# Relative bias rows of both sample attentions: loaded in the prompt attention from the Pool queue and kept on chip

## The reference, cut to what matters

```
bias = jnp.moveaxis(bias_tab[rel_bucket(jnp.maximum(dist, 0))], -1, -2)
logit = jnp.einsum('nqhe,nqkhe->nqhk', q, kg) + bias
p = jax.nn.softmax(logit, axis=-1)
return jnp.einsum('nqhk,nqkhe->nqhe', p, vg)
```

## Time and profile before

| what | value |
|---|---|
| median of the runs | 3127.01 us (3124.59 to 3127.49) |
| the profiled execution | 3129.59 us, of which the span is 3127.8 us |
| PE busy | 2659.0 us (85% of the span) |
| DVE / ACT / POOL busy | 1136.5 / 666.8 / 366.8 us |
| PE's share of the chain that ended last | 40% (the MLP, at the end) |
| prompt attention | 1251 to 1449 us, PE busy 166.18 us of 198 |
| sample attention B | 1449 to 1589 us, PE busy 79.74 us of 140 |
| sample attention C | 1589 to 1834 us, PE busy 160.65 us of 245 |

### The profile page before, as it was taken

The page is one execution under the profiler, slowest core; times in us unless marked ns, Lnnn a source line. Parts: engine busy times, 40 slices in busy tenths (PEclk is TensorE's granted clock), DMA queues, the critical chain, the costliest instruction groups (busy, mean ns, idle before and its releaser), DMA issues. The chain is left out here.

```text
span 3127.8 us, 33968 instructions
## 1 busy us (share of the span) xinstructions
PE 2659.0 (85%) x13588; PEld 1692.1 (54%) x13604; DVE 1136.5 (36%) x2070; ACT 666.8 (21%) x1346; POOL 366.8 (12%) x352
## 2 busy tenths in 40 slices
PE   7999995085788987886638769999999999999998
PEld 3444442032667776454425434566666666888843
DVE  0007999655666665484615202100000000000033
ACT  1122221032334544574303200100000000000011
POOL 1000000101444431000016520000000000000000
PEclk9999997576799999798768879999999999999999
DMA  6111110241335532414779772301101113110010
GB/s 238 51 42 51 41 41 20 100 114 39 112 97 161 150 126 77 155 38 131 254 216 359 284 269 101 115 27 40 40 27 40 40 28 105 39 38 29 11 34 33
DMA packets 170291, 305.86 MB, mean 98 GB/s; under 512 B 48536, under 2 KB 121448, under 8 KB 167866
## 3 DMA queue, kind: packets, MB, share of 16 engines
q1 hardware_dynamic: 145154, 175.87, 18.0%
q0 software_dynamic: 23136, 93.01, 8.2%
q10 hardware_dynamic: 1864, 35.08, 3.3%
HBM read 262.76 MB, written 68.29 MB: 106 GB/s over the span
## 5 line engine op out<-in xcount | busy, mean ns | idle before, releaser
L929 PE MATMUL m_B<-m_big,m_wdB 128*128 128x363 f32 (+1 forms) x2112 | 646.1, 468 | 3.2 <-issue 3.2
L929 PEld LDWEIGHTS m_B<-m_big,m_wdB 128*128 128x128 f32 x2112 | 400.4, 190 | 248.0 <-issue 5.0
L384 PE MATMUL i_psM<-i_w,i_xnT 128*128 128x477 f32 x1024 | 418.3, 567 | 2.3 <-ACT i_xnT L232 2.3
L384 PEld LDWEIGHTS i_psM<-i_w,i_xnT 128*128 128x128 f32 x1024 | 192.8, 191 | 213.5 <-issue 206.5
L791 DVE TENSOR_TENSOR m_actT<-m_wdB,m_B 128x363 f32 (+3 forms) x66 | 35.1, 532 | 604.1 <-PE m_B L929 604.1
L683 ACT ACTIVATE m_wdB<-m_B 128x363 f32<-128x363 f32 (+1 forms) x66 | 31.2, 473 | 599.0 <-PE m_B L929 599.0
L971 PE MATMUL m_B<-m_wdA,m_actT 128*128 128x256 f32 x704 | 152.4, 379 | 0.8 <-DVE m_actT L791 0.8
L971 PE MATMUL m_B<-m_wdB,m_actT 128*128 128x256 f32 x704 | 152.6, 379 | 0.0
L971 PEld LDWEIGHTS m_B<-m_wdA,m_actT 128*128 128x128 f32 x704 | 133.7, 190 | 19.5 <-DVE m_actT L791 1.4
L971 PEld LDWEIGHTS m_B<-m_wdB,m_actT 128*128 128x128 f32 x704 | 133.5, 190 | 18.8 <-issue 0.8
L649 POOL TENSOR_TENSOR m_rstd<-m_ms,m_half 128x1 f32<-128x1 f32 x18 | 9.9, 553 | 1133.3 <-DVE m_ms L759 1133.3
(11 more groups left out here) (414 smaller groups left out, 3587.0 us busy)
## 6 DMA issues: line engine op xcount, KB each, us to landing
b_Kp<-b_k SPq DMA_DIRECT2D x32, 512.0 KB, 10.5
b_Vp<-b_v SPq DMA_DIRECT2D x32, 512.0 KB, 11.2
o_bk<-b_k ACTq DMA_DIRECT2D x8, 2040.0 KB
o_bv<-b_v ACTq DMA_DIRECT2D x8, 2040.0 KB
i_w<-w_in POOLq DMA_DIRECT2D x8, 1908.0 KB, 29.9
proj<-i_stage SPq DMA_DIRECT2D x64, 238.5 KB, 2.0
m_wdB<-w_gate SPq DMA_DIRECT2D x22, 512.0 KB, 4.0
m_wdB<-w_up SPq DMA_DIRECT2D x22, 512.0 KB, 5.2
```

The lines of the kernel that those rows point to most:

```text
L384: mm = nc.tensor.matmul(psM[:, c % 2, 0:CHW], xnT[:, t % 2, k, :], w[:, k, c * CHW:(c + 1) * CHW], start=(k == 0), stop=(k == KO - 1))
L929: mm = nc.tensor.matmul(B[:, bank, 0:r1 - r0], wgu[:, i, u, k, :], hnT[:, k, r0:r1], start=(k == 0), stop=(k == KO - 1))
```

## The change

The bias tiles become objects (`Relative`) that are made before the prompt attention: `near` for B, `far` for C. Both are filled inside `phase_prompt` by POOL, which first waits until the prompt's eight table loads have landed. The 32 + 32 DMAs are the same in shape, source and target as before; only their queue and place differ. `load_bias` is gone from ACT's list in B and from SP's in C. DVE's wait stays where it was and now waits for the semaphore of the object. `sample_c` is no phase of its own any more: C's block follows B's inside `attend`, while `far` is still allocated.

```diff
-def phase_prompt(nc, D, kth):
+def phase_prompt(nc, D, kth, rels):
...
+            @block.gpsimd
+            def _(pool):
+                for h in range(8):
+                    pool.wait_ge(table_in[h], 16)
+                for rel in rels:
+                    rel.load(pool, D)
...
-def phase_sample(nc, D, sparse, kth=None):
+def phase_sample(nc, D, sparse, rel, kth=None):
...
-        bias = sb("bias", [P, TOT])
+        bias = rel.tile
...
-            def load_bias(eng):
-
-                for n in range(4):
-                    for tok in range(DEC):
-                        h0, y = 4 if sparse else 0, FAR - KEYS - tok
-                        eng.dma_start(bias[32 * n + tok:32 * n + 32:DEC, :],
-                                      D["table"][h0:h0 + 4, y:y + TOT]).then_inc(S["bias_in"], 16)
...
                     load_small(sp)
-                    load_bias(sp)
                     load_late(sp)
...
                     load_small(act)
-                    load_bias(act)
                     load_late(act)
...
-                        dve.wait_ge(S["bias_in"], 16 * 4 * DEC)
+                        dve.wait_ge(rel.loaded, 16 * 4 * DEC)
...
+class Relative:
+
+
+    def __init__(self, nc, ctx, tag, keys, head):
+        self.keys, self.head = keys, head
+        self.tile = ctx.enter_context(nc.sbuf_tensor(tag + "_bias", [P, keys + DEC], F32))
+        self.loaded = nc.alloc_semaphore(tag + "_bias_in")
+
+    def load(self, eng, D):
+
+        for n in range(4):
+            for tok in range(DEC):
+                y = FAR - self.keys - tok
+                eng.dma_start(self.tile[32 * n + tok:32 * n + 32:DEC, :],
+                              D["table"][self.head:self.head + 4, y:y + self.keys + DEC]).then_inc(self.loaded, 16)
...
 def phase_attend(nc, D):
 
-    with ExitStack() as ctx:
-        kth = Kth(nc, lambda n, s, dt=F32: ctx.enter_context(nc.sbuf_tensor(n, s, dt)), "k_", S_HALF + DEC)
-        phase_prompt(nc, D, kth)
-        phase_sample(nc, D, False, kth)
-
-
-def phase_sample_c(nc, D):
-    phase_sample(nc, D, True)
+    with ExitStack() as outer:
+        far = Relative(nc, outer, "c", PAST, 4)
+        with ExitStack() as ctx:
+            near = Relative(nc, ctx, "b", WB, 0)
+            kth = Kth(nc, lambda n, s, dt=F32: ctx.enter_context(nc.sbuf_tensor(n, s, dt)), "k_", S_HALF + DEC)
+            phase_prompt(nc, D, kth, (near, far))
+            phase_sample(nc, D, False, near, kth)
+        phase_sample(nc, D, True, far)
```

More of the change, by code:

```diff
@@ L2607, in phase_sample @@
         pad_stored = sem("pad_stored")
-        names = "bias_in keysT products logit nmx prob probT PT pv newT PTn out_new rden on picked out stored own".split()
+        names = "keysT products logit nmx prob probT PT pv newT PTn out_new rden on picked out stored own".split()
         S = {n: sem(n) for n in names}
@@ L3161 @@
 PHASES = {"input": phase_input, "mix": phase_mix, "attend": phase_attend,
-          "sample_c": phase_sample_c, "mlp": phase_mlp}
+          "mlp": phase_mlp}
 def mix_constants(a):
```

## The result

The changed kernel takes 3111.36 us in the median (3108.58 to 3112.5), 0.9949 of the kernel before (95% interval 0.9935 to 0.9962). That is 15.7 us faster, a third of the 44.8 that were forecast, and outside the range of 3070 to 3100. The profiled execution took 3110.31 us, with a span of 3108.5.

The account below looks back on a forecast made before the run. Engines were taken to wait at the starts of B and C for bias loads and keys. Terms -15 - 31 - 0.8 + 2 = -44.8 us took the median 3127.01 to 3082.2 us, range 3070 to 3100.

Parts of the forecast that it names:

- B, -15: Start of sample attention B: without the 32 loads in ACT's list everything moves up, -15 us, range -11.4 to -20.7.
- the meeting, -0.8: Between B and C: one of two meetings of phases goes, -0.8 us.
- C, -31: Start of sample attention C: gathers without bias rows land sooner and pieces are turned faster, -31 us, range -27.2 to -34.7.
- Rival 2: C's start: gathers are slow by themselves, only DVE's 12.7 us go there; 3100.5 us in all, chance 0.07.
- DVE beside POOL's issues, +1 of 0 to 2.2: Prompt attention: DVE runs slower while POOL issues the 64 loads, +1 us, 0 at best, 2.2 at most.
- Rival 4: Prompt attention: POOL's issues hold up DVE's logits on the chain, so the kernel gets slower, 3140 us; chance 0.04.
- rival 3: B and C: the change moves nothing, since the waits named after the bias ended with something else; 3127 us, chance 0.04.
- The DMA engines in the prompt, +1 of 0 to 9.9: Prompt attention: the moved loads fall on the transfer of `p_V` and delay it, +1 us, range 0 to +9.9.
- rival 1: Prompt attention: `p_V` and `p_rows` come late, giving back part of the gain, 9.9 in place of 1; 3091 us, chance 0.10.

## Why the prediction failed, step by step

- **B, -15, and the meeting, -0.8.** Right: -16.8 together. The 11.4 us of ACT went, the wait for the 17th piece stayed (12.6 us), values were issued 18.0 us into the block (1495.85) as forecast, and the fourth chunk's logits came 51 us into it (1528.81), forecast 51. DVE's idle time ahead of them grew to 8.3 us, not 12.
- **C, -31.** Right in size and in the main mechanism: -31.7, the first product at 23.4 us into the block (21 to 24 forecast), pieces 1.3 us apart. The split was off, and two misses cancel in part: the first piece is turned 12.8 us into the block (1614.43) in place of 14.9, 2.1 us earlier where 4.1 to 6.1 were forecast, and from there to the first product it takes 10.6 us in place of 38.9, -28.3 at the better end of 23.1 to 28.6. Rival 2, gathers slow by themselves, falls by this and by the wider loads in the old place.
- **DVE beside POOL's issues, +1 of 0 to 2.2.** The low end: with the loads after `p_V` the prompt is 0.1 us longer than before and DVE's busy time the same. Rival 4 falls with it, and rival 3 by the gains of B and C. The lock between DVE and GpSimd that the Trainium skill describes (SBUF — State Buffer, section "SBUF: two separate sides") does not show on these issues; the section ties it to certain DVE operations, those in a 2-port mode, and those with two SBUF inputs while GpSimd reads SBUF, and no run here tells which of the prompt's are of that kind.
- **The DMA engines in the prompt, +1 of 0 to 9.9.** This step failed, and it alone: it measured 29.3. It is rival 1's mechanism, which stood at 0.10, but at three times the price, so that not even the rival's 3091 was near. Two things in the step were wrong. The bound said "had `p_V` to wait behind all of them" and counted B's rows only, because 64 issues were reckoned at 80 us, 1.25 us each, from the gather; then C's rows would have come too late to meet `p_V`. POOL issues this shape in 0.518 us, C's first load goes out at 1283.1, and C's rows alone cost 20.7 us (B's rows alone cost 9.4, close to the bound, though that was reckoned from ACT's pace, so in part by luck). And the value +1 came from total load, "1.03 MB of rows in 40 us" over all engines, where the row that bore on it was in hand: in the earlier trace rows the rows moved 0.46 MB in 10 us and, on only 2.7 engines' worth of time, cut the gathers to half. I used that for C's gain and not for the prompt's price, although it is the same collision with another victim. At that rate, as an estimate from that row, C's 2.10 MB alone would have been some 45 us beside other traffic, an upper end which would have put "slower" into the range.
- **The rule of the Trainium skill** (DMA: Bandwidth & Descriptors, section "Why a DMA increments its semaphore by 16 and not by 1"), that a load of four rows from GpSimd runs on engines that rotate, would have made the prompt's DMA term nothing. The trace does not bear it out: with the engines 26% busy and `p_V` outstanding for 20 us more, twelve engines stood idle, which a rotation would have used. That loads of more rows use more engines agrees (0.99 busy with 16 rows).
- **The sum.** With the one term replaced, -15 - 31 - 0.8 + 1 + 29.3 = -16.5; measured -15.7. With the collision removed by one wait the kernel takes 3080.04 us, where 3082.2 was forecast for the change itself.

## What to carry to other kernels

A load with few long rows does not need many bytes to hurt: it fills a few DMA engines, and every wide transfer that has a share on those engines comes as late as they let it, while the average said here that the engines were a quarter busy. So when loads are moved into an "idle" stretch, list every transfer that is outstanding there with the wait that hangs on it, and hold the moved loads back until the last urgent one has landed; here one wait on POOL was worth 31 us. And where one row of the profile shows a collision that the change removes, use that same row to price the collision it may create.

## What the runs showed of the hardware that was not expected

- POOL issues a direct load in 0.518 us (four rows) or 0.483 us (16 rows, median of 8), about half of its gather's 0.938.
- Four engines full and twelve idle can hold PE for 29.3 us: on those four, in 10 us, 0.92 MB of long rows went past for 0.11 MB in packets of `p_V`, two packets of 1 KB for each of 16,416 bytes.
- Long rows into 16 partitions kept all 16 engines busy (0.99) at 215 GB/s, half of the 407 that pieces over 128 partitions reach; a row took 1.16 us where it took 0.62 on four engines. The cause stays open.
